# Router bias as a TensorE product, maxima read from PSUM, and three residual products placed behind the first expert's hidden products

## The reference, cut to what matters

```python
x = layer_norm(DN_ALPHA * x + memory_cross_attention(...), ln_xa_g[layer], ln_xa_b[layer])
# hierarchical_moe(x, wg, bg, we, be, w1, w3, w2)
g_logits = xf @ wg + bg                       # 4 groups
g_star = argmax(g_logits)
p_group = softmax(g_logits)[g_star]
e_logits = einsum('td,dge->tge', xf, we) + be # 4 groups of 8 experts
e_logits = e_logits[g_star]
top_val, top_idx = top_k(e_logits, 2)
gate = p_group * softmax(top_val)
# each token goes to its two experts: (silu(x w1[e]) * (x w3[e])) w2[e], weighted by gate
x = layer_norm(DN_ALPHA * x + moe, ln_ffn_g[layer], ln_ffn_b[layer])
```

## Time and profile before

| | us |
|---|---|
| median of 3 runs | 1407.27 |
| lowest and highest | 1405.2, 1407.91 |
| the profiled execution | 1405.65 |
| its span, first to last instruction | 1403.8 |
| PE busy | 1143.7 (81%) |
| DVE busy | 396.3 (28%) |
| ACT busy | 169.5 (12%) |
| POOL busy | 28.2 (2%) |
| DMA | 477.43 MB, mean 340 GB/s |

### The profile page before, as it was taken

How to read it: one execution, slowest core, us unless ns; L and a number is a source line. 1 busy time by engine, 2 the same in 40 slices (tenths; PEclk the granted TensorE clock), 3 DMA queues, 4 the chain that set the end, 5 groups by cost and what they waited for, 6 DMA issues and landing times.

```text
span 1403.8 us, 33059 instructions
## 1 busy us (share of the span) xinstructions
PE 1143.7 (81%) x11866; PEld 727.6 (52%) x11867; DVE 396.3 (28%) x1046; ACT 169.5 (12%) x473; POOL 28.2 (2%) x77
## 2 busy tenths in 40 slices
PE   8999999988996786758789999999897767667664
PEld 7885448554553443434448867655454434334332
DVE  1872622252231121112122223252222111111113
ACT  1112511111110010000011001111110000000001
POOL 3000000000000000000000000000000000000000
PEclk9999999999998898888899999999999888888887
DMA  9856308489999999999996647455999999999994
GB/s 333 256 180 240 120 30 330 180 319 413 429 428 428 430 428 428 430 427 430 428 410 257 240 168 323 183 214 222 411 427 430 428 427 431 427 429 429 427 430 206
DMA packets 68825, 477.43 MB, mean 340 GB/s; under 512 B 8284, under 2 KB 15740, under 8 KB 43948
## 3 DMA queue, kind: packets, MB, share of 16 engines
q1 hardware_dynamic: 66732, 470.27, 81.8%
q0 software_dynamic: 2048, 6.51, 1.3%
HBM read 473.62 MB, written 3.15 MB: 340 GB/s over the span
## 4 chain that ended last, share of the span: by engine, by line
PE 55%; DMA 27%; SPq 7%; issue 4%; DVE 2%; another core or an unknown queue 2%; ACT 1%; ACTq 1%; POOL 0%; DVEq 0%
DMA ring<-in_moe_w_dram 17%; PE bank L554 13%; PE bank L990 11%; DMA slot<-in_moe_w_dram 10%; PE bank L575 8%; SPq L465 7%; PE bank L1006 4%; PE bank L1014 3%; PE bank L976 2%; PE bank L756 2%; PE bank L562 2%; PE bank L524 1%; PE bank L877 1%; PE bank L997 1%
## 5 line engine op out<-in xcount | busy, mean ns | idle before, releaser
L990 PE MATMUL bank<-ring,xT 128*32 128x256 f32 x1920 | 178.6, 451 | 41.7 <-DMA ring<-in_moe_w_dram 41.7
L990 PE MATMUL bank<-slot,xT 128*32 128x256 f32 x1120 | 160.9, 449 | 10.2 <-issue 10.2
L554 PE MATMUL bank<-xT,ring 128*128 128x256 f32 x720 | 157.1, 379 | 0.7 <-PE bank L554 0.7
L554 PEld LDWEIGHTS bank<-xT,ring 128*128 128x128 f32 x720 | 136.3, 190 | 19.4 <-issue 1.1
L990 PEld LDWEIGHTS bank<-ring,xT 128*32 128x32 f32 x1920 | 91.8, 129 | 80.6 <-issue 59.8
L990 PE MATMUL bank<-spare,xT 128*32 128x256 f32 x512 | 81.8, 490 | 61.6 <-DMA ring<-in_moe_w_dram 61.4
L1537 DVE SCALAR_TENSOR_TENSOR xT<-xT,bank 64x256 f32<-64x256 f32 x73 | 30.3, 415 | 355.1 <-ACT xT L1780 355.1
L990 PE MATMUL bank<-held,xT 128*32 128x256 f32 x608 | 88.6, 455 | 47.1 <-DMA slot<-in_moe_w_dram 47.1
L575 PE MATMUL bank<-ring,slot 128*128 128x512 f32 x256 | 111.5, 593 | 4.0 <-ACT slot L1754 2.0
L1006 PE MATMUL bank<-ring,xT 128*32 128x256 f32 x1824 | 109.1, 379 | 2.1 <-DVE xT L1547 2.0
L1014 PE MATMUL bank<-xT 32*128 32x256 f32 x1200 | 87.8, 407 | 21.0 <-issue 19.7
(11 more groups left out here) (283 smaller groups left out, 1087.6 us busy)
## 6 DMA issues: line engine op xcount, KB each, us to landing
ring<-in_moe_w_dram SPq DMA_DIRECT2D x96, 2048.0 KB, 47.2
slot<-in_moe_w_dram SPq DMA_DIRECT2D x48, 2048.0 KB, 48.3
held<-in_moe_w_dram SPq DMA_DIRECT2D x16, 2048.0 KB, 40.7
spare<-in_moe_w_dram SPq DMA_DIRECT2D x16, 2048.0 KB, 47.3
gains<-in_moe_w_dram SPq DMA_DIRECT2D x16, 2048.0 KB, 47.4
ring<-in_od_w_in_dram SPq DMA_DIRECT2D x6, 2048.0 KB, 20.8
ring<-in_xa_wq_dram SPq DMA_DIRECT2D x4, 2048.0 KB, 11.5
ring<-in_xa_wo_dram SPq DMA_DIRECT2D x4, 2048.0 KB, 11.6
```

The costliest lines, as they stand in the source:

```text
L554: ins = mm(ps, w[:, k, c0:c0 + P], rhs[:, k, :], start=(k == 4), stop=(k == 3))
L990: ins = mm(b1[qs[2 * m + h], 0:S], xg[:, k, :], ws[m][:, k, h, :, :], start=(k == 0), stop=(k == KC - 1))
```

## The change

The bias becomes a product of one row (`ones` by `rbias`) that opens the logits' sum; `wr` and `rbias` get 40 columns, of which columns 4 to 7 are zero and -1e30, so that the maximum over 8 columns can be taken from PSUM. `logits(t)` takes bank 5 + t instead of the rotation's next. DVE reads the maxima from PSUM, and compares integers instead of converting them. Tile 0's whole router work stands behind the plain rows of tile 1. ACT takes the exponentials from PSUM, and drains the banks of the logits; the exponents are made on DVE before the counts instead of behind them. The waits for banks 5 and 6 and `start_sum(1..3, 1)` change their places. GpSimd sets the padding and an integer ramp `number`, and loads the bias to one partition.

```diff
@@ -46,6 +46,7 @@
 EPG = 8
 NE = NG * EPG
 CAP = 32
+RG, RW = 8, 8 + NE
 Q = 4
 ROUNDS = S // CAP
 RING = 6
@@ -146,14 +147,13 @@
         round_caps = sb("round_caps", [P, ROUNDS])
         cols = sb("cols", [P, C_ALL])
         lngT = sb("lngT", [P, LN_COUNT, 2, KC])
-        wr = sb("wr", [P, DEPTH, KC, NG + NE])
-        rbias = sb("rbias", [P, DEPTH, NG + NE])
+        wr = sb("wr", [P, DEPTH, KC, RW])
+        rbias = sb("rbias", [1, DEPTH, RW])
 
         lg = sb("lg", [P, TT, NG, EPG])
-        g8 = sb("g8", [P, TT, 8])
         top = sb("top", [P, TT, 2, 8])
         topi = sb("topi", [P, TT, 2, 8], U32)
-        topf = sb("topf", [P, TT, 2, 8])
+        number = sb("number", [P, NE], U32)
         other = sb("other", [P, TT, NG])
         e01 = sb("e01", [P, TT, 2, NE])
         cw = e01[:, :, :, :].rearrange("p t m e -> p (t m e)")[:, 0:TAPS * CC]
@@ -390,7 +390,7 @@
             load_cols("mk1", T["mem_wk"], 512)
             for L in range(DEPTH):
                 sp.dma_start(wr[:, L, :, 0:NG], T["moe_wg"][L].rearrange("(p k) g -> p k g", k=KC)).then_inc(router_loaded, 16)
-                sp.dma_start(wr[:, L, :, NG:NG + NE], T["moe_we"][L].rearrange("(p k) g e -> p k (g e)", k=KC)).then_inc(router_loaded, 16)
+                sp.dma_start(wr[:, L, :, RG:RW], T["moe_we"][L].rearrange("(p k) g e -> p k (g e)", k=KC)).then_inc(router_loaded, 16)
             for b, n in enumerate(("ev_cmp_w1_k", "ev_cmp_w1_v")):
                 load(f"c{b}", lambda r: r.rearrange("p (j n) -> p j n", j=16),
                      T[n][0].rearrange("(j p) n -> p j n", p=P))
@@ -926,11 +926,13 @@
                 def logits(t, warm=0):
 
                     pe.wait_ge(router_loaded, 16 * 2 * DEPTH)
-                    ps = claim(pe, ("lg", L, t))
+                    ps = claim(pe, ("lg", L, t), bank=5 + t)
                     keep_warm(ps, warm)
+                    pe.wait_ge(bias_loaded, 32)
+                    mm(ps[:, 0:RW], ones[0:1, :], rbias[0:1, L, :], start=True, stop=False)
                     for k in AS_TURNED:
                         fresh_part(3 * L + 1, k, t)
-                        ins = mm(ps[:, 0:NG + NE], xT[:, k, t * P:(t + 1) * P], wr[:, L, k, :], start=(k == 4), stop=(k == 3))
+                        ins = mm(ps[:, 0:RW], xT[:, k, t * P:(t + 1) * P], wr[:, L, k, :], start=False, stop=(k == 3))
                     filled(ins, ("lg", L, t))
 
                 logits(0)
@@ -963,8 +965,6 @@
                 ins.then_inc(counted, 1)
                 pe.wait_ge(x_ready[1], 3 * L + 2)
                 start_sum(0, 1)
-                for b in (5, 6):
-                    pe.wait_ge(bank_drained[b], fills[b])
                 pe.wait_ge(bank_drained[4], fills[4])
                 rotation[0] = 4
                 qs = [slice(q * CAP, (q + 1) * CAP) for q in range(Q)]
@@ -1021,8 +1021,6 @@
                 pe.wait_ge(units_of_ready, L + 1)
                 mm(bY[0:1, 64:64 + NE], units_of[:, :], ident[0:NE, 0:NE], start=True, stop=True)
                 mm(bY[0:1, 64 + NE:64 + 2 * NE], units_of[:, :], tri[0:NE, 0:NE], start=True, stop=True).then_inc(first_ready, 1)
-                for q in range(1, Q):
-                    start_sum(q, 1)
 
                 def unit_hidden(s, ready, n):
 
@@ -1048,7 +1046,11 @@
 
                     return [(i + (moe_base[L][s] + 1)) * 16 for s in moe_slots[L][j]]
 
+                for b in (5, 6):
+                    pe.wait_ge(bank_drained[b], fills[b])
                 unit_hidden(moe_slots[L][0], ready_at(0, 0), 1)
+                for q in range(1, Q):
+                    start_sum(q, 1)
                 pe.wait_ge(units_ready, L + 1)
                 with nc.Fori(0, TURNS, engines=[pe.engine], head_slot={pe.engine: 0}) as i:
                     def expert(j):
@@ -1114,7 +1116,7 @@
                     ins.then_inc(xT_by_dve, 1)
             drained(ins, (("n", i), t, 1))
 
-        def norm_dve(st, v, i, between=None, behind=None):
+        def norm_dve(st, v, i, behind=None):
 
             if i == 0:
                 v.wait_ge(small_loaded, 16 * 8)
@@ -1142,19 +1144,12 @@
             to_xT(st, v, i, 0)
             gain_bias(st, v, i, 0)
             stats(1, 1)
-            if between is None:
-                plain(1)
-                to_xT(st, v, i, 1)
-            else:
-                st.wait()
-                row_rstd(v, i, 1, 2)
-                between()
-                v.wait_ge(ln_rstd, 2 * i + 2)
-                nc.vector.tensor_scalar(x[:, 1, :], x[:, 1, :], mv[:, 1, 0:1], rstd[:, 1, :], ALU.subtract, ALU.mult).then_inc(n_ready, 1)
+            plain(1)
+            if behind is not None:
                 behind()
-                to_xT(st, v, i, 1)
-                return
-            gain_bias(st, v, i, 1)
+            to_xT(st, v, i, 1)
+            if behind is None:
+                gain_bias(st, v, i, 1)
 
         MOE_ORDER = (2, 3, 0, 1)
         LAST_NORM = LN_COUNT - 1
@@ -1251,7 +1246,6 @@
             nc.vector.memset(zero16[:, :], 0.0).then_inc(zero_ready, 1)
             nc.vector.memset(aT[:, :, 0:PAD], 0.0)
             nc.vector.memset(blocks[:, :, :, :, :], 0.0)
-            nc.vector.memset(g8[:, :, :], NEG)
             st.do(nc.vector.memset(pc[:, :, :, :], 0.0))
             zeros_set = st.n
             for t in range(TT):
@@ -1464,23 +1458,18 @@
                     drained(cp(probT[:, h % 2, 0, :, :], ps[:, :].rearrange("p (m s) -> p m s", m=2)), ("xp", L, h))
                 fam = families[L]
 
-                def group_logits(t):
-
-                    if t == 0:
-                        v.wait_ge(bias_loaded, 32)
+                def best_group(t):
+
                     ps = wait_filled(v, ("lg", L, t))
-                    st.do(tt(g8[:, t, 0:NG], ps[:, 0:NG], rbias[:, L, 0:NG], ALU.add))
-                    drained(tt(lg[:, t, :, :], ps[:, NG:NG + NE].rearrange("p (g e) -> p g e", g=NG),
-                               rbias[:, L, NG:NG + NE].rearrange("p (g e) -> p g e", g=NG), ALU.add), ("lg", L, t))
-                    st.do(nc.vector.max(top[:, t, 0, :], g8[:, t, :]))
-                    st.do(nc.vector.max_index(topi[:, t, 0, :], top[:, t, 0, :], g8[:, t, :]))
+                    st.do(nc.vector.max(top[:, t, 0, :], ps[:, 0:RG]))
+                    st.do(nc.vector.max_index(topi[:, t, 0, :], top[:, t, 0, :], ps[:, 0:RG]))
 
                 def one_group(t):
 
-                    st.do(cp(topf[:, t, 0, 0:1], topi[:, t, 0, 0:1]))
-                    st.do(ts(other[:, t, :], iota[:, 0:NG], topf[:, t, 0, 0:1], NEG, ALU.not_equal, ALU.mult))
-                    wait_drained(v, ("lg", L, t))
-                    st.do(tt(lg[:, t, :, :], lg[:, t, :, :], other[:, t, :].unsqueeze(2).to_broadcast([P, NG, EPG]), ALU.add))
+                    st.do(tt(other[:, t, :], number[:, 0:NG], topi[:, t, 0, 0:1].to_broadcast([P, NG]), ALU.not_equal))
+                    ps = banks[bank_of[("lg", L, t)][0]]
+                    st.do(stt(out=lg[:, t, :, :], in0=other[:, t, :].unsqueeze(2).to_broadcast([P, NG, EPG]), scalar=NEG,
+                              in1=ps[:, RG:RW].rearrange("p (g e) -> p g e", g=NG), op0=ALU.mult, op1=ALU.add))
 
                 def two_best(t):
 
@@ -1490,20 +1479,20 @@
 
                 def two_experts(t):
 
-                    st.do(cp(topf[:, t, 1, 0:2], topi[:, t, 1, 0:2]))
-                    st.do(tt(e01[:, t, :, :], iota[:, 0:NE].unsqueeze(1).to_broadcast([P, 2, NE]),
-                             topf[:, t, 1, 0:2].unsqueeze(2).to_broadcast([P, 2, NE]), ALU.is_equal))
+                    st.do(tt(e01[:, t, :, :], number[:, :].unsqueeze(1).to_broadcast([P, 2, NE]),
+                             topi[:, t, 1, 0:2].unsqueeze(2).to_broadcast([P, 2, NE]), ALU.is_equal))
                     tt(mask[:, t, :], e01[:, t, 0, :], e01[:, t, 1, :], ALU.add).then_inc(mask_ready, 1)
 
                 def first_tile():
 
+                    best_group(0)
                     one_group(0)
                     two_best(0)
 
-                norm_dve(st, v, 3 * L + 1, lambda: group_logits(0), first_tile)
+                norm_dve(st, v, 3 * L + 1, first_tile)
                 two_experts(0)
                 multiplied = gain(st, v, 3 * L + 1, 1)
-                group_logits(1)
+                best_group(1)
                 one_group(1)
                 two_best(1)
                 two_experts(1)
@@ -1561,10 +1550,10 @@
                 drained(stt(out=place[:, :, :], in0=pv, scalar=1.0, in1=mask[:, :, :], op0=ALU.add, op1=ALU.mult), ("pos", L))
                 wait_drained(v, ("pos", L))
                 build(0, 0)
+                exponents()
                 v.wait_ge(counted, L + 1)
                 st.do(tt(beyond[:, :], banks[7][0:NE, 0:ROUNDS], round_caps[0:NE, :], ALU.is_gt))
                 nc.vector.tensor_reduce(units_of[:, :], beyond[:, :], AX, ALU.add).then_inc(units_of_ready, 1)
-                exponents()
                 st.do(nc.vector.memset(comb, 0.0))
```

(15 more changed lines are left out.)

## The result

The changed kernel takes 1412.42 us (median of 5 runs, 1410.91 to 1415.3) against 1407.16 for the kernel before (5 runs, 1405.2 to 1407.91): ratio 1.0043, with a 95% interval of 1.0031 to 1.0056. It is slower by some 5 to 6 us; the forecast was slower by 1.5. The profiled execution took 1410.91, its span 1409.1, so 5.3 more than before.

What follows compares the result with a forecast made beforehand. The weight stream was taken to bound the kernel, its gaps hanging on TensorE after the router. Layer 0's 0.6 and layer 1's 0.9 us gave 1407.27 + 1.5 = 1408.8 us, range 1405.2 to 1411.8.

Steps and rivals of the forecast that it cites:

- the sum: Both layers' delays added: layer 0 0.1 + 0.5 = 0.6, layer 1 0.1 + 0.8 = 0.9, together +1.5 us.
- the third rival: PE's stands around the router lower the granted clock; 3 to 4 us in each layer, about 1416; chance 0.04.
- the second: Slower: layer 1's entry into the expert loop pauses 4.56 us like layer 0's instead of 0.79; 1411.8; chance 0.12.
- What bounds the kernel: MoE weight stream sets the pace; its gaps hang on TensorE's progress after the router, and delays carry to the layer's end.
- First part: logits(0) in bank 5 waits for L1128's readout until 288.95; transposes of tile 1 start at 292.47, +0.31 us.
- Second part: logits(1) in bank 6 waits for ACT's readout with the six zero products queued behind; logits begin at 296.31, +1.86 us.
- Third part: Behind the logits the wait for L1473 goes; PE's zeroing and residual products put positions at 300.68, +1.19 us.
- the shorter DVE chain: Tile 1's DVE chain loses 0.64 us, but mask 1 is ready 0.5 us ahead of PE, so it is off the path.
- that cover: Exponentials, which drain banks 5 and 6 and hold the hidden products, are done some 0.5 us before take.
- Fourth part: start_sum(1..3, 1) behind the hidden products: these start +0.1 us; passes ahead of scatter cost 0.5 in layer 0, 0.8 in layer 1.
- The first rival: Faster: the bank waits don't bind, hidden products 1.3 us earlier; layer 1 -0.5, layer 0 -0.8, 1406.0; chance 0.19.

Runs made afterwards that it cites:

- free-banks experiment: Changed kernel with logits(0) in bank 6, tile 1's transposes in 7 and 0, logits(1) in 5: median 1408.88 us, ratio 1.0013.
- the later runs: The changed kernel unaltered, run once more beside the kernel before: 9 executions, median 1416.48 us, ratio 1.0058.

## Why the prediction was wrong

Two things that the sum put at nothing failed it: the fall of the clock behind the wait for bank 5, which was the third rival at 0.04, and the pause at layer 1's entry, the second at 0.12. In the profiled execution only the first came, and it made 1.67 of the 5.3 us. The terms that the sum did have, for waits, bias products and passes, were right in kind and too small: 2.6 where 1.5 was forecast. Another 0.6 of the 5.3 lies ahead of the two stages and 0.5 at the end.

**What bounds the kernel** was right: the stage's delay at SP's issues in each layer came through to the end.

**First part, bank 5.** The wait was right: `logits(0)` at 289.45 - 0.46 = 288.99, forecast 288.95. Layer 1 has the transposes +0.48 instead of +0.31, because the bias product takes 0.31 to 0.34 and not 0.22, and the handoff from DVE 0.10 and not 0.06. In layer 0 the step failed by the clock: transposes at 294.68 - 0.46 = 294.22 where 292.47 was forecast, 1.75 later. I had weighed the fall as a rival with a chance of 0.04, from a window in which TensorE stands still and the clock still reads 1.00. That was the wrong row: here the lower clock showed only behind the standing still. The kernel before has it right behind its pause in layer 0:

```profile
312.00:313.00 1.00, 1.00 (x12) 0.92 (x16) 0.92 (x4) 0.00 (x0) 0.00 (x0) 0.51 1.05 442
```

I had its price as 3 to 4 us in each layer, over a stretch from 296 on. It was 1.67, from 291.4 to 294.8, in one layer of two: from the logits' start to the six zeros it took 7.60 us in layer 0 and 5.93 in layer 1.

**Second part, bank 6.** Right in place and size: the zeros begin 2.37 (layer 0) and 2.29 (layer 1) behind the first transpose, forecast 2.32.

**Third part.** Positions: forecast +1.19, layer 1 has +1.57 (947.32 - 3.52 against 942.23). Of the 0.38 too many, 0.17 had come with the first part and 0.2 with the zeros and the second bias product. As forecast the shorter DVE chain buys nothing; mask 1 was ready at 302.68, the positions started at 303.18. Reading PSUM and comparing integers cost no more than the operations that they replaced: from the first maximum (300.79) to the start of the bias addition on `x` (302.59) it was 1.80, forecast 1.90. The exponentials were done at 305.3, before `take` at 306.30; that cover held.

**Fourth part.** Hidden products: forecast +0.1; layer 1 has 950.65 - 3.52 = 947.13, +0.6. `take` and hidden products followed the positions. The passes behind them took 1.49 in both layers. In layer 0 the pause went from 4.56 to 3.72, so 0.65 of them were net, forecast 0.5. In layer 1 the pause went from 0.79 to 0 in this execution, forecast 0.8 for the net and 0.7 measured. Layer 1's `scatter` came 1.3 later (955.73 - 3.52 against 950.90), forecast 0.9.

**The rivals.** The second, a long pause at layer 1's entry, is real: 3 us in six of the thirteen profiles with products behind. I gave it 0.12 as a thing that either is or isn't, where it comes in some executions and not in others: its mean belongs into the sum. I took it as 4.56 us long; it was 3.0, but the lower clock behind it, which I hadn't counted, brought it to 4.6. The pause from which it decides was also wrong: by the terms of the sum, 0.6 + 0.1 + (pause - 0.8) passes 2.8 at 2.9 us, not at 3.3. The first rival, banks not binding, was the free-banks experiment, for which it said 1406.0; the profiled execution without a pause took 1404.23, the one with it 1408.88.

**In sum**, for both layers: waits, bias and passes 1.3 in layer 1 and 2.94 - 1.67 = 1.3 in layer 0, so 2.6 (forecast 1.5); the clock at the router 7/12 x 1.65 x 2 = 1.9 on average (forecast nothing); the pause 6/13 x 3.06 = 1.4 and the lower clock behind it 5/13 x 1.6 = 0.6 (forecast nothing). That gives 6.5, beside 5.3 between the first medians and 9.5 between those of the later runs (8.2 by its ratio). The shares of 7/12 and 6/13 are counts of few profiles, over several versions of the kernel. An execution with both falls and the pause would lose 2.6 + 3.3 + 4.6 = 10.5. With that and the scatter of the kernel before (1403.19 to 1409.86 in the same session), the highest executions can be reached. Part of this scatter lies ahead of the change: the output projection before layer 0's router ends anywhere from 286.6 to 291.0 us in the twenty profiles. Why the later median is so high stays open, as does what decides in which execution the clock falls or the block comes late.

## What to carry to other kernels

A number in a claim can cost more than the work that the change saves: before a bank is fixed by hand, write down who held it last and when it is read out, and what stands behind the claim in the same queue. Products that keep TensorE busy belong ahead of the wait, not behind it. When a prediction hangs on an event that executions draw, put its mean into the sum, and profile the same program more than once before a single profile is believed.

## What the runs showed of the hardware that was not expected

TensorE's clock fell to its lower level after a stand of only 0.8 to 1.0 us ahead of the narrow logits' products, in 7 of 12 stages, and never at the router in the 28 stages without that; the seven products behind it then took 2.93 to 3.19 us instead of 1.68. Behind a stand of 1.23 to 1.25 us elsewhere in the router it fell in none of 12 stages, and behind a pause of 3 us at layer 1's loop in five of six, which cost 1.6 us more. A block of instructions of 16384 bytes came ahead of a 2 MB weight transfer in every profile with a pause of 0 to 0.79 us at that entry, and in the middle of it in every one with 3 us; the same program showed both. A maximum over 8 columns took DVE 0.17 us from PSUM and 0.16 from SBUF.
